# Thirty-two experts of a mixture layer: loop replaced by written-out code, weight stream reordered, outputs summed in PSUM, one of twelve weight units multiplied in plain fp32

## What is computed

```python
logits = (h @ w_router + b_router).astype(F32)
top_logit, top_idx = lax.top_k(logits, TOP_K)          # 4 of 32
top_p = jax.nn.softmax(top_logit, axis=-1)
...
gu = xb @ w_gu[e] + b_gu[e]                            # 1024 x 2048 per expert
glu = jnp.minimum(gu[:, :D_EXPERT], SWIGLU_LIMIT)
```

## Time and profile before

| | us |
|---|---|
| median of 3 runs | 4019.8 (4016.48 to 4021.62) |
| profiled execution | 4024.09 |
| its span in the trace | 4022.3 |
| expert stage, first `pick` (line 1588) to last `yT` add (line 1596) | 1320.4 to 2636.1 |

### The profile page before, as it was taken

One profiled execution on the slowest core, in us unless ns is written; L12 is line 12 of the kernel. 1 busy time (PEld: TensorE's weight loads), 2 busy tenths in 40 slices (PEclk: granted clock), 3 DMA queues, 4 the chain that ended last, 5 costly groups with the idle time before them and its releaser, 6 DMA issues. The chain is left out here.

```text
span 4022.3 us, 51270 instructions
## 1 busy us (share of the span) xinstructions
PE 3078.3 (77%) x17216; PEld 2524.4 (63%) x17217; DVE 2429.5 (60%) x3532; ACT 1645.2 (41%) x2098; POOL 752.9 (19%) x272
## 2 busy tenths in 40 slices
PE   7689999888676788888888888838336987625788
PEld 2368888566476667666767676728224987622688
DVE  1235545343354798989898989845544554454555
ACT  0024444211132576767777777713111442211343
POOL 0022232000000344444544454500000000000000
PEclk9789999877787899999999999969556998755899
DMA  7241100111141888888888888733001542200443
GB/s 261 76 76 32 32 22 1 34 35 59 46 150 49 329 319 315 303 319 302 323 301 321 303 320 299 250 105 111 1 1 51 159 167 84 79 0 0 141 142 104
DMA packets 323602, 605.74 MB, mean 151 GB/s; under 512 B 21858, under 2 KB 79769, under 8 KB 323353
## 3 DMA queue, kind: packets, MB, share of 16 engines
q1 hardware_dynamic: 318300, 598.43, 43.3%
q10 hardware_dynamic: 5181, 5.76, 0.5%
HBM read 599.75 MB, written 4.39 MB: 150 GB/s over the span
## 5 line engine op out<-in xcount | busy, mean ns | idle before, releaser
L1488 POOL TENSOR_TENSOR moe_raw_r<-moe_raw,moe_hi 128x2048 fp32r<-128x2048 f32 x96 | 609.5, 6349 | 1306.3 <-ACT moe_hi L1699 1306.3
L1699 ACT ACTIVATE moe_hi<-moe_raw 128x2048 fp32r<-128x2048 f32 x384 | 708.9, 1903 | 1.9 <-DMA moe_raw<-in_w_gu 1.5
L1488 DVE TENSOR_TENSOR moe_raw_r<-moe_raw,moe_hi 128x2048 fp32r<-128x2048 f32 x288 | 681.5, 2393 | 29.0 <-DVE acs L1627 19.2
L1522 PE MATMUL banks<-moe_hi,moe_xs 128*128 128x512 f32 x1024 | 410.1, 400 | 34.7 <-DVE moe_raw_r L1488 27.7
L1523 PE MATMUL banks<-moe_raw_r,moe_xs 128*128 128x512 f32 x1024 | 401.2, 392 | 0.0
L1522 PE MATMUL banks<-moe_hi,acs 128*128 128x512 f32 x512 | 248.8, 486 | 169.1 <-DVEq L1630 121.0
L319 PE MATMUL banks<-ff_xs,ff_hi 128*128 128x272 f32 x1024 | 300.9, 294 | 70.3 <-DVE ff_raw_r L335 61.0
L321 PE MATMUL banks<-ff_xs,ff_raw_r 128*128 128x272 f32 x1024 | 298.5, 291 | 0.0
L320 PE MATMUL banks<-ff_xs,ff_hi 128*128 128x272 f32 x1024 | 298.0, 291 | 0.0
L1522 PEld LDWEIGHTS banks<-moe_hi,acs 128*128 128x128 f32 x512 | 119.7, 234 | 222.3 <-issue 134.4
L1522 PEld LDWEIGHTS banks<-moe_hi,moe_xs 128*128 128x128 f32 x1024 | 193.3, 189 | 96.0 <-DVE moe_raw_r L1488 41.7
(11 more groups left out here) (471 smaller groups left out, 6553.2 us busy)
## 6 DMA issues: line engine op xcount, KB each, us to landing
moe_raw<-in_w_gu SPq DMA_DIRECT2D x256, 1024.0 KB, 7.9
moe_raw<-in_w_down SPq DMA_DIRECT2D x128, 1024.0 KB, 5.1
ff_raw<-in_w_ff SPq DMA_DIRECT2D x128, 512.0 KB, 3.8
ring_mod<-in_w_mod SPq DMA_DIRECT2D x12, 2048.0 KB, 8.7
wq<-in_w_in SPq DMA_DIRECT2D x32, 512.0 KB, 4.1
ring_att<-in_w_in SPq DMA_DIRECT2D x32, 512.0 KB, 3.7
ring_att<-in_w_in SPq DMA_DIRECT2D x32, 448.0 KB, 3.7
wh<-in_w_in SPq DMA_DIRECT2D x10, 1024.0 KB, 8.5
```

The source lines that it names most:

```text
L1488: eng.tensor_tensor(rest[u][:, :, :], raw[u][:, :, :], hi[:, u % HI_SLOTS, :, :].bitcast(F32), ALU.subtract).then_inc(sem, 1)
L1522: pe.matmul(bank, x[:, k, :], hi[:, u % HI_SLOTS, k, :], start=first, stop=False)
L1699: act.activation(hi[:, u % HI_SLOTS, :, :], raw[u][:, :, :], ACT.Copy).then_inc(his, 1)
```

## The change

- The loop is gone: all 32 experts are written out, and semaphores are waited for against constants. `preload_act_table` loads the sigmoid table once, ahead.
- The stream is reordered. In units: gate `g(e+1)` q0 to q3, then `d(e)` q0 to q3, then up `u(e+1)` q0 to q3. A unit is now 256 whole rows of 1024 columns. PE, ACT and DVE each follow this order, with the activations of an expert worked on while PE has `g` of the next one.
- The first twelve units are loaded in `route`, as soon as its own three loads are issued.
- Tokens are split once, in `route` (`h_hi`, `h_lo`: two ACT copies and two DVE subtractions of 128 x 1024 in place of four copies), and the gather is 32 fp32r matmuls with 64 columns; the result is copied by ACT in one piece.
- `turn` is a matmul in plain fp32 with the constant `fold`, which transposes and adds the two halves at once. DVE's second add goes.
- Gates are no longer in the one-hot matrix: `slots_of` turns `pick` and gets each slot's gate with a one-column matmul, and ACT scales the output with it. `pickg` goes.
- Outputs stay in PSUM: banks 4 to 7 collect `b_down` and all scatters (fp32, moving operand 512 columns), and DVE's adds go. At the end a new stage copies them and turns them back.
- Unit `d(e)` q2 isn't split. PE multiplies `raw` as it has landed with the fp32 activations `g`, in four plain fp32 matmuls of 64 stationary and 512 moving columns. Eleven of twelve units are split, all by ACT and DVE; POOL has no work.

```diff
+def stream_order():
+    out = [("g", 0, q) for q in range(4)] + [("u", 0, q) for q in range(4)]
+    for e in range(NEXP):
+        if e + 1 < NEXP:
+            out += [("g", e + 1, q) for q in range(4)]
+        out += [("d", e, q) for q in range(4)]
+        if e + 1 < NEXP:
+            out += [("u", e + 1, q) for q in range(4)]
+    return out
...
+    split = [n for n, (ph, e, q) in enumerate(order) if (ph, q) != ("d", 2)]
+    nth = {n: i for i, n in enumerate(split)}
...
+        def gather(pe, hot_one, bank):
+            for k in range(KT):
+                for x, c in ((h_hi, 0), (h_lo, SLOTS)):
+                    for t in range(2):
+                        ins = pe.matmul(ps[bank + k // 4][:, k % 4 * P + c:k % 4 * P + c + SLOTS], x[:, t, k * P:(k + 1) * P],
+                                        hot_one[:, t, 0:SLOTS], start=(t == 0), stop=(t == 1))
...
+                def unit(ph, e, q):
+                    n = place[ph, e, q]
+                    x = (acs if ph == "d" else xs[:, e % 2])[:, 2 * q:2 * q + 2, :]
+                    if n not in nth:
+                        pe.wait_ge(loaded[n % UNITS], n // UNITS * 16 + 16)
+                        for k in range(2):
+                            for c in range(2):
+                                ins = pe.matmul(ps[pair(e) + c][0:SLOTS, :], g[:, 0, k, :],
+                                                raw[n % UNITS][:, k * D + c * 512:k * D + c * 512 + 512],
+                                                start=False, stop=False)
+                        ins.then_inc(used, 1)
+                        return
+                    pe.wait_ge(los, nth[n] + 1)
+                    for k in range(2):
+                        for w, first, last in ((hi[nth[n] % HI_SLOTS], q + k == 0, False), (rest[n % UNITS], False, q + k == 4)):
+                            for c in range(2):
+                                ins = pe.matmul(ps[pair(e) + c][:, :], x[:, k, :], w[:, k * D + c * 512:k * D + c * 512 + 512],
+                                                start=first, stop=last)
+                    ins.then_inc(used, 1)
+                def fetch(e):
+                    pe.wait_ge(hot, e + 1)
+                    gather(pe, pick[:, e % 2], pair(e)).then_inc(gath, 1)
+                def slots_in(e):
+                    slots_of(pe, pick[:, e % 2], lambda t: gate[:, t, e:e + 1], pair(e + 1)).then_inc(slots, 1)
+                def turn(e, h):
+                    for s in range(2):
+                        for m in range(4):
+                            ins = pe.matmul(ps[pair(e) + h][:, (4 * s + m) * SLOTS:(4 * s + m + 1) * SLOTS],
+                                            gs[:, s, (4 * h + m) * P:(4 * h + m + 1) * P], fold, start=True, stop=True)
+                    ins.then_inc(turned, 1)
+                def scatter(e):
+                    pe.wait_ge(y_out, e + 1)
+                    for t in range(2):
+                        for c in range(2):
+                            ins = pe.matmul(ps[4 + 2 * t + c][:, :], pickT[:, t * P:(t + 1) * P], y[:, c * 512:(c + 1) * 512],
+                                            start=False, stop=(e == NEXP - 1))
+                    ins.then_inc(scat, 1)
...
+                for e in range(NEXP):
+                    nxt = e + 1 < NEXP
+                    if nxt:
+                        pe.wait_ge(x_out, e + 2)
+                        for q in range(2):
+                            unit("g", e + 1, q)
+                    turn(e, 1)
+                    if nxt:
+                        for q in range(2, 4):
+                            unit("g", e + 1, q)
+                    pe.wait_ge(t_free, 2 * e + 2)
+                    for q in range(4):
+                        if q % 2 == 0:
+                            pe.wait_ge(act_ready, 2 * e + q // 2 + 1)
+                        unit("d", e, q)
+                    if nxt:
+                        pe.wait_ge(gu_out, 2 * e + 3)
+                        for q in range(4):
+                            unit("u", e + 1, q)
+                            if q == 1:
+                                scatter(e)
+                            if q == 2:
+                                slots_in(e + 1)
+                        if e + 2 < NEXP:
+                            pe.wait_ge(s_out, e + 2)
+                            fetch(e + 2)
+                        pe.wait_ge(gu_out, 2 * e + 4)
+                        turn(e + 1, 0)
+                    else:
+                        scatter(e)
...
+                for e in range(NEXP):
+                    nxt = e + 1 < NEXP
+                    g0, d0, u0 = place.get(("g", e + 1, 0)), place["d", e, 0], place.get(("u", e + 1, 0))
+                    if nxt:
+                        rounded(g0)
+                        if e:
+                            results(e - 1)
+                        for q in range(1, 4):
+                            rounded(g0 + q)
+                    elif e:
+                        results(e - 1)
+                    slots_out(e)
+                    rounded(d0)
+                    out("u", e)
+                    rounded(d0 + 1)
+                    if nxt:
+                        x_of(e + 1)
+                    rounded(d0 + 2)
+                    sigmoid(e, 0)
+                    rounded(d0 + 3)
+                    if nxt:
+                        rounded(u0)
+                        out("g", e + 1)
+                        rounded(u0 + 1)
+                    sigmoid(e, 1)
+                    if nxt:
+                        rounded(u0 + 2)
+                        rounded(u0 + 3)
...
+                for e in range(NEXP):
+                    nxt = e + 1 < NEXP
+                    g0, d0, u0 = place.get(("g", e + 1, 0)), place["d", e, 0], place.get(("u", e + 1, 0))
+                    if nxt:
+                        lo(g0, g0 + 1)
+                    act_first(e, 0)
+                    if nxt:
+                        lo(g0 + 2)
+                    act_second(e, 0)
+                    if nxt:
+                        lo(g0 + 3)
+                    act_first(e, 1)
+                    lo(d0)
+                    act_second(e, 1)
+                    lo(d0 + 1, d0 + 2, d0 + 3)
+                    if nxt:
+                        lo(u0)
+                        if e + 2 < NEXP:
+                            dve.wait_ge(slots, e + 1)
+                            hot_of(e + 2)
+                        lo(u0 + 1, u0 + 2, u0 + 3)
...
+                pe.wait_ge(h_split, 2)
+                for t in range(2):
+                    for c in range(2):
+                        pe.matmul(ps[4 + 2 * t + c][:, :], gT[:, t * P:(t + 1) * P], bd[:, c * 512:(c + 1) * 512],
+                                  start=True, stop=False)
```

More of the change, by code:

```diff
@@ L1440, in experts @@
     NJ = RMAX * E_N
+    order = stream_order()
+    place = {unit: n for n, unit in enumerate(order)}
+    split = [n for n, (ph, e, q) in enumerate(order) if (ph, q) != ("d", 2)]
+    nth = {n: i for i, n in enumerate(split)}
+    w_gu, w_down = a["w_gu"][0], a["w_down"][0]
     with contextlib.ExitStack() as ctx:
@@ new lines, in experts @@
+        over_loads = " ".join(f"o_w{u}" for u in range(UNITS))
+        over_names = ("o_hot o_gath o_x o_used o_his o_los o_gu_out o_turned o_t_free o_glu o_sig o_act_ready o_gcol o_gt_mm "
+                      "o_gt_out o_y_out o_sc_mm o_added o_act_v")
+        with stage(nc, over_names + " " + over_loads) as (block, hot, gath, x_out, used, his, los, gu_out, turned, t_free, glu,
+                                                          sig, act_ready, gcol, gt_mm, gt_out, y_out, sc_mm, added, act_v,
+                                                          *loads):
+            ACT_STEPS = 12
@@ L1571, in body @@
                         products(i, u, ps[6 + u % 2][:, :], acs[:, (u - 8) // 2 * 4:(u - 8) // 2 * 4 + 4, :])
-                    if not ahead:
-                        scatter(i)
-                if ahead:
-                    gather(0)
-                over(pe, body)
-                if ahead:
-                    scatter(NEXP)
+                    pe.wait_ge(y_out, i + 1)
+                    for r in range(4):
+                        for m in range(2):
+                            k = 2 * r + m
+                            ins = pe.matmul(ps[4 + r][:, m * LAT:(m + 1) * LAT], y[:, k * P:(k + 1) * P], pickT[:, :],
+                                            start=True, stop=True)
+                        ins.then_inc(sc_mm, 1)
+                further(pe, body)
             @block.vector
@@ L1911, in _ @@
                 act.activation(pr[:, :, :], pr[:, :, :], ACT.Exp).then_inc(on_act, 1)
+                for t in range(2):
+                    act.wait_ge(mm, 3 + t)
+                    act.activation(h_hi[:, t, :].rearrange("p (b n) -> p b n", b=2), ps.all[:, 3 + 2 * t:5 + 2 * t, :],
+                                   ACT.Copy).then_inc(h_act, 1)
             @block.tensor
```

426 lines of the change are left out of this document (231 added, 195 removed).

## The result

The changed kernel takes 4199.7 us at the median (4197.8 to 4201.7) against 4020.2: ratio 1.0448, 95% interval 1.043 to 1.0466. The forecast was 4090 with a range of 3990 to 4145, so the direction was right and the size was not: the cost is 180 us, not 70. The profiled execution took 4198.4 us, its span 4196.6.

What follows compares the result with a forecast made beforehand. DVE was nearest its limit; after the change the path through the program orders binds: 40.45 us per expert plus 2.15 for the clock, 42.6 over 32 experts, line 1773 70 us later, hence 4090 us (range 3990 to 4145).

Steps and rivals of the forecast that it cites:

- the clock term: PE around its wait before d q1: the fall to 1.2 GHz adds 2.15 us per expert, period 42.6.
- the first bias add: DVE's start on the first expert's activations: first turn at 1357.5 us, DVE 0.43 us after PE's last turn instruction.
- The path: Program orders across PE, ACT and DVE in one expert: period 40.45 us at full clock, what it was before.
- the sigmoid's wait: DVE stands 1.85 us because half 1's sigmoid queues on ACT behind the gate-product copy and a rounding.
- The split of a unit: DVE's subtraction for one unit: 2.25 us with POOL resting, where the mean was 2.393.
- The plain unit is no gain: Unit d q2 unsplit puts 3.44 us on PE's path instead of 1.81; DVE's saved 2.25 falls where it waits.
- Gather and load rule: Gather of 32 matmuls at 0.107 us, 3.4 in all (1.7 to 3.7); fast non-FP32 weight loads would give the lower bound.
- Rival 1: PE's clock doesn't fall, or the gather is cheap: period 39.65 to 40.45, time 3996 to 4021 us; chance 0.15.
- Rival 2: Engine loads set the expert stage's pace: period 35 to 37, at 36 a time of 3879 us; chance 0.15.
- Rival 3: Written-out expert code starves PE of instructions: at 2 us an expert, 4155 us; chance 0.08.
- rival 4: The change doesn't do what it says, as if overflow experts ran a second pass; chance below 0.01.
- Early loads: First twelve loads issued in route: worth 0, up to 3 us, since ACT starts on them only behind the gather.

Runs made afterwards that it cites:

- e1: Changed kernel with each gather matmul widened from 64 to 128 moving columns by zeros, same count and fp32r type: 4093.5 us, ratio 1.0186 to the kernel before.
- e6: e5 with the 128-column gather of e1: 3870.2 us, ratio 0.963 to the kernel before.
- e8: Changed kernel with the 128-column gather of e1 and all twelve units split, so no plain fp32 unit: 4078.3 us, ratio 1.0146 to the kernel before.
- e5: Changed kernel with half 1's sigmoid earlier on ACT and three DVE subtractions ahead of the activation chain: 3928.2 us, ratio 0.9785 to the kernel before.
- e10: e6 with the first twelve loads issued at the start of the expert stage, not in routing: 3877.1 us, ratio 0.9655 to the kernel before.
- e3: Changed kernel with half 1's sigmoid on ACT moved ahead of the gate-product copy and a rounding: 4002.9 us, ratio 0.9963 to the kernel before.
- e11: Kernel before the change with its plain fp32 gather narrowed from 128 to 64 moving columns: 4017.8 us, ratio 1.000 to the kernel before.
- e12: Changed kernel with its 64-column gather in plain fp32 instead of fp32r: 4226.0 us, ratio 1.0523 to the kernel before.
- e2: Changed kernel with unit d q2 split like the other eleven, so no plain fp32 unit: 4104.5 us, ratio 1.0215 to the kernel before.

## Why the prediction was right and wrong

**The step that failed is the clock term.** "PE's wait of 3.9 us follows one of 1.65 and a burst of one unit: much as before" gave 2.15 us of work for an expert, and the fall it describes came: e1, where it is alone, has 3.41 us at 1.2 GHz, 1.7 of work. But I looked for falls only where PE waits. The gather's 32 matmuls were costed by their distance (0.112 us against my 0.107) and not asked what they do to the clock, so a second fall was put at nothing. It came, and both stretches together cost 5.5 to 6.0 us of work where I had 2.15; taking the second away, in e1, gives 46.08 - 42.67 = 3.41 us of period back. The account: 32 x (46.08 - 42.6) = 111 us; the first bias add, at 1354.04, 3.9 earlier than forecast (1357.5 + 0.43), since the stage began at 1315.94 and not at 1320.4; the rest -2. Line 1773 of before, 1974 of after, starts at 2820.91 where I had 2715.0, 106 later. (The terms that lead to my 1357.5 add up to 1356.9, a slip of 0.6.)

```profile
1354.04 0.69 DVE L1718 TENSOR_TENSOR gu<-banks,vec 128x512 f32<-128x512 f32 x1 [5.53 <-PE banks L1575]
...
2820.91 3.25 DVE L1974 SCALAR_TENSOR_TENSOR xT<-moe_yT,modT,xT 128x256 f32<-128x256 f32 x8 [9.10 <-PEq L163]
```

No row of before could have told: the form wasn't there. I bounded its duration from both sides but not its effect on the clock. The range should have held one more low stretch per expert, which at 3.4 to 6.8 us costs half of that, 32 times: 54 to 109 us, up to 4200. That width is known only with hindsight.

**The path** held: 40.1 to 40.6 against 40.45. Its waits came where they were put, but longer: DVE 12.4 us before the first bias add (forecast some 8), the sigmoid's wait 2.96 (1.85), PE's 4.65 before `d` q1 (3.9). In e1, where the clock is full at the gather and the turn, they are 10.4, 2.1 and 3.7. So the second fall makes 2.0 of DVE's 12.4 us; the other 2.4 over the forecast are not explained. The split of a unit was sized right at 2.285 (2.25). So were the scatter and the plain unit at full clock: of eight recorded instructions of 0.59 us they take 3.60 (e1) and 3.65 (e6), which puts them (3.60 - 0.59) / 7 = 0.43 and 0.44 apart, 3.44 and 3.5 for eight (3.44).

**"The plain unit is no gain"** is right in sign, but 1.6 was too much: at full clock e8 puts it at 0.9 to 1.1. In after itself it costs 3.0, most of it by way of the clock, for which I have no mechanism.

**Gather and load rule.** The distance of 0.112 us is close to the upper bound (0.117), and a recorded weight load of line 1511 takes 192 ns at the median, where fp32 took 194 on the mean. By the rule of the Trainium skill (TensorE: Matmul & The Clock Gate, section on weight-path perf modes), if it counted fp32r as not FP32, the distance would have been near 0.05 by the prediction's estimate. With fp32r counted so the trace doesn't agree, and the measurement decides.

**The rivals.** Rival 1, the clock doesn't fall, is out, as it fell twice. Rival 2, the loads set the pace, gave 3879 for a period of 36 and named its condition: ACT's copy and rounding must not hold the sigmoid, and PE must not stand for long. e5 meets it by its orders and takes 3928; with the wide gather too, e6, it is 3870 and a period of 35.51. So the change as written didn't meet the rival's condition, and its 3879 came near. What then sets the pace is PE's work, not the transfer of the weights. Rival 3, code starving PE, is out: e6 is written out too and PE is busy 100%. Of rival 4 nothing shows.

**Early loads**, costed at 0 with 3 as the upper end, are worth 4.2 us inside the stage by e10. I had taken ACT's start behind the gather as the cover; it hides the first three units, and for most of those from the fourth on ACT waits 0.5 to 0.9 us. This was measured on the orders of e6, not on the change itself.

**The first fall.** In before, in after and in e1, waits of PE of 3.7 to 5.2 us went with a fall in every expert; that of 1.6 us in e3 did not, and no wait between was tried. The Trainium skill (TensorE: Matmul & The Clock Gate, section on HAM oscillation) warns of bursts of matmuls shorter than the wait for the next data, which start at the low clock. For this fall the trace agrees, with waits for DVE in the place of waits for DMA: in e1 one unit of some 2 us lies between the waits of 1.29 and 3.73 us.

## What to carry to other kernels

Ask of a new form of matmul two questions, how long it takes and what it leaves the clock at; a full PE doesn't answer the second, and only the granted clock of a window does. Where every engine is under its limit, write out one period of the program orders before anything is cut: here shorter loads won nothing, and moving one sigmoid and a few subtractions took 272 us off the changed kernel. A sum of the path is worth the trouble, for it tells which one instruction to move.

## What the hardware showed that I had not expected

- PE's clock falls to 1.2 GHz with PE 100% busy, in or behind a run of 32 fp32r matmuls of 64 columns, 0.112 us apart (window 1626 to 1633 of after: busy 7.00 of 7.00, clock 0.51). With 128 columns at the same distance it doesn't (e1), nor with 64 columns in plain fp32 (e11, e12). It doesn't fall at every gather: in e3 in 16 of 24 experts, and in e5, where PE has no wait in the expert, it is at 1.2 GHz for 2.56 us per expert. What in fp32r with 64 columns makes the difference was not tried.
- Widening each gather matmul by 64 columns of zeros gave back 106 us; the distance of the matmuls stayed the same.
- After a fall the low clock lasted some 3 us in some experts and some 7 in others of the same kernel; splitting the plain unit made the long ones rare in one kernel (after to e2, 36 of 48 to 3 of 39) and brought them up in another (e1 to e8, 0 of 24 to 9 of 24). What decides the length is open.
